# Two-block kernel: the context's norm spread over the second feed-forward layer, its root taken with Ln and Exp

## Chip, cores and metric

One Trainium2 chip, one core of it. The metric is the device time of one execution in microseconds (us), the median over several runs.

## What is computed

One launch computes two model blocks behind each other: a first block of two layers (a retention mixer and a feed-forward layer, then a recurrent mixer and a feed-forward layer) and a second block (state-space mixer with a Fourier branch, then a mixture of experts). The feed-forward layers and the context's norm, which the change touches, are these:

```python
def swiglu_ffn(x, w_in, w_out):
    gate, up = jnp.split(x @ w_in, 2, axis=-1)
    return (jax.nn.silu(gate) * up) @ w_out
...
def rmsnorm(u, w):
    uf = u.astype(jnp.float32)
    uf = uf * lax.rsqrt(jnp.mean(uf * uf, axis=-1, keepdims=True) + EPS)
    return uf.astype(u.dtype) * w

def modulate(u, shift, scale):
    return u * (1 + scale) + shift
...
        prj_c = modulate(rmsnorm(ctx, norm1[layer]), sh1c, sc1c) @ w_in[layer]
```

The sequence and the context have 256 tokens each, the model width is 1024, the feed-forward width 2816 (22 tiles of 128 rows each for gate and for up).

## The kernel before, in words

Each engine has its program written out by hand, and the engines meet at semaphores. Activations lie transposed: the width on the 128 partitions in eight tiles, the 256 tokens as columns. SyncE streams the weights through a ring of 2 MB slots.

**Split products.** An fp32 product is made of three passes. For each chunk of weights (128x1024, eight 128x128 blocks) ScalarE rounds it to `w_hi` (`weights_hi`, line 1545), VectorE forms the remainder `w_lo` (`weights_lo`, line 2038), and TensorE multiplies hi by hi, hi by lo and lo by hi. There are three sets of `w_hi` and `w_lo`: the rounding of chunk n waits until TensorE is done with chunk n-3. In the feed-forward layers one chunk is one 128-row tile of the output.

**The feed-forward layer** (`ffn` in each engine's program: lines 913, 1628 and 2220). The products of `w_in` go to PSUM in 22 out tiles of 128x512, `TILE["ffn_in1", 0]` to `21`, two chunks each, over six banks: the even ones are gates, the odd ones ups. For each pair j, VectorE reads the gate tile 2j out of PSUM, makes two remainders, reads the up tile 2j+1, multiplies it by the gate's Silu (`act<-act,work`), copies the product to `hid_hi` (`CAST`), forms `hid_lo`, and goes on with two more remainders. ScalarE does the Silu of pair j and then the roundings of the next four chunks. Each read of a tile raises `bank_read` of its bank. The first eight chunks' worth of tiles (0 to 3) come out together at the start, the products looping over the input there (`outer_gemm`).

**The context.** GpSimd squares the context `cx` (128x2048) and adds the eight tiles of squares up (lines 641 to 646), in four instructions that start when the sums of squares of the layer's input are done. In the second layer TensorE sums over the partitions with a product by ones in front of chunk 14, ScalarE takes a `Sqrt` ahead of the Silu of pair 4 (line 1633), VectorE a reciprocal ahead of the gate of pair 5 (line 2229), and GpSimd multiplies `cx` by it, four instructions in a row (line 650). ScalarE applies scale and shift and rounds (`context_hi`, line 1618) at pairs 6 to 9, and GpSimd forms the remainders `ctx_lo` behind it (line 653). The context's products come after the feed-forward layer.

The lines of the instructions in the trace are those of helpers: 690 for every product, 1455 for ScalarE, 2001 for VectorE's tensor_tensor.

Of the kernel before, what the change touches and what calls it, by code (L numbers as in the profile page):

```python
# [35 lines left out]
ALU = mybir.AluOpType  # L36
# [3 lines left out]
P = 128  # L40
T = 256
# [197 lines left out]
def two_blocks(nc, a, out):  # L239

    ctx = ExitStack()
    with ctx:
# [54 lines left out]
        def col(name, i=0, n=1, rows=P):  # L297
            return vec[0:rows, VOFF[name][0] + i:VOFF[name][0] + i + n]
# [57 lines left out]
        def xs_both(m):  # L356
# [60 lines left out]
            "ones_set", "csil_zero", "csil_ready", "w_hi_ready", "w_lo_ready", "chunk_used", "in_hi_ready", "in_lo_ready",  # L417
            "sq_ready", "osq_ready", "osum_ready", "sum_ready", "silu_ready", "hid_ready", "gy_ready", "pool_ready", "pool_step", "stats_full", "rstd_ready", "scaled_ready", "h_ready", "x_ready", "rope_done",
            "omv_ready", "osd_ready", "pads_zero", "uc_ready", "tap_ready", "lsp_dve", "lsp_act", "a_ready",
            "th_ready", "lsq_arg", "lsq_ready", "g_done", "go_hi_ready", "go_ready", "mod_full", "wt_ready", "ctx_sum", "ctx_full", "ctx_dev", "ctx_rstd", "ctx_v", "ctx_w", "ctx_hi_ready", "ctx_lo_ready", "coef_ready", "wdt_hi_ready", "wdt_lo_ready", "center_ready", "x_mod",  # L420
            "dt_dve", "dt_act", "dt_ready", "xw_ready", "xd_ready", "rl_ready", "cl_ready", "ce_ready", "dec_ready",
            "m_ready", "y_ready", "exp_arg", "exp_ready", "msk_ready", "count_full", "route_ready", "moe_init",
            "eq_ready", "sgb_ready", "gath_full", "xg_ready", "sg_full", "sgt_ready", "sc_full", "sc_free", "gu_full", "gs_ready",
# [183 lines left out]
        def _(pool):  # L607
            steps = [0]

            def settle(x):  # L610

                x.then_inc(s["pool_step"], 1)
                steps[0] += 1
                pool.wait_ge(s["pool_step"], steps[0])

            def sum_squares(i):

                for j in range(1, 4):
                    pool.wait_ge(s["sq_ready"], 4 * i + j + 1)
                    settle(pool.tensor_tensor(out=sq2[:, 0:2, :], in0=sq2[:, 0:2, :], in1=sq2[:, 2 * j:2 * j + 2, :],  # L620
                                              op=ALU.add))
                pool.tensor_tensor(out=sq2[:, 0, :], in0=sq2[:, 0, :], in1=sq2[:, 1, :], op=ALU.add).then_inc(
                    s["sum_ready"], 1)
# [13 lines left out]
            for j in range(KL):  # L637
                await_read(pool, TILE["lru_u", j] if j < KL // 2 else TILE["lru_y", j - KL // 2])
                v = upad[:, 2 * j:2 * j + 2, LPAD:] if j < KL // 2 else gy[:, 2 * j - KL:2 * j - KL + 2, :]
                pool.tensor_tensor(out=v, in0=v, in1=rstd2, op=ALU.mult).then_inc(s["pool_ready"], 1)  # L640
            pool.wait_ge(s["sum_ready"], 4)
            pool.wait_ge(s["ld_ctx"], 16)
            settle(pool.tensor_tensor(out=sqc, in0=cx, in1=cx, op=ALU.mult))
            settle(pool.tensor_tensor(out=sqc[:, 0:4, :], in0=sqc[:, 0:4, :], in1=sqc[:, 4:8, :], op=ALU.add))
            settle(pool.tensor_tensor(out=sqc[:, 0:2, :], in0=sqc[:, 0:2, :], in1=sqc[:, 2:4, :], op=ALU.add))
            pool.tensor_tensor(out=sqc[:, 0, :], in0=sqc[:, 0, :], in1=sqc[:, 1, :], op=ALU.add).then_inc(s["ctx_sum"], 1)
            pool.wait_ge(s["ctx_rstd"], 1)
            for j in range(4):
                c2 = cx[:, 2 * j:2 * j + 2, :]
                pool.tensor_tensor(out=c2, in0=c2, in1=lnb.unsqueeze(1).to_broadcast([P, 2, T]), op=ALU.mult).then_inc(s["ctx_v"], 1)  # L650
            for j in range(4):
                pool.wait_ge(s["ctx_hi_ready"], 2 * j + 2)
                pool.tensor_tensor(out=ctx_lo[:, 2 * j:2 * j + 2, :], in0=cx[:, 2 * j:2 * j + 2, :],
                                   in1=ctx_hi[:, 2 * j:2 * j + 2, :].bitcast(F32), op=ALU.subtract).then_inc(s["ctx_lo_ready"], 1)
            sum_squares(4)
            pool.wait_ge(s["mod_full"], len(MOD_GROUPS))
            pool.dma_start(wr[0], a["wroute"][:, 0:4, :]).then_inc(s["ld_route"], 16)
# [19 lines left out]
        def _(pe):  # L677
# [233 lines left out]
            next_input(1, "ffn_in0", (1,))  # L911

            def ffn(layer):
                split_gemm(f"ffn_in{layer}", 14, KD, in_hi, in_lo, first_m=BPC)
                if layer:
                    pe.wait_ge(s["ctx_sum"], 1)
                    mm(ps[:, STAT, T:2 * T], ones[:, :], sqc[:, 0, :], True, True, s["ctx_full"])
                split_gemm(f"ffn_in{layer}", 2 * KF, KD, in_hi, in_lo, first_m=14)
                split_gemm(f"ffn_out{layer}", KD, KF, hid_hi, hid_lo,
                           lambda c: pe.wait_ge(s["hid_ready"], KF // 2 * layer + c // 2 + 1))  # L920

# [529 lines left out]
        def _(act):  # L1451
            steps = [0]

            def fn(o, i, f, inc=None, **kw):
                x = act.activation(o, i, f, **kw)  # L1455
                if inc is not None:
                    x.then_inc(inc, 1)
                return x
# [169 lines left out]
            def ffn(layer):  # L1628
                for j in range(KF // 2):
                    weights_hi(chunks_by(f"ffn_in{layer}", 2 * j))  # L1630
                    if layer and j == 4:
                        act.wait_ge(s["ctx_full"], 1)
                        fn(lnb, ps[:, STAT, T:2 * T], ACT.Sqrt, s["ctx_dev"], scale=1.0 / D, bias=col("eps"))
                    if layer and 6 <= j < 10:
                        context_hi(j - 6)
                    await_read(act, TILE[f"ffn_in{layer}", 2 * j])
                    fn(act2[:, j % 2, :], act2[:, j % 2, :], ACT.Silu, s["silu_ready"])
                mixer_out(f"ffn_out{layer}", lambda j: weights_hi(chunks_by(f"ffn_out{layer}", j)))
# [352 lines left out]
        def _(dve):  # L1991
# [228 lines left out]
            def ffn(layer):  # L2220
                for j in range(KF // 2):
                    tg, tu = TILE[f"ffn_in{layer}", 2 * j], TILE[f"ffn_in{layer}", 2 * j + 1]
                    hid, hi = cut(act2[:, j % 2, :], 2, T), hid_hi[:, 2 * j:2 * j + 2, :]
                    weights_lo(chunks_by(f"ffn_in{layer}", 2 * j))
                    if layer and j == 2:
                        modulation()
                    if layer and j == 5:
                        dve.wait_ge(s["ctx_dev"], 1)
                        dve.reciprocal(lnb, lnb).then_inc(s["ctx_rstd"], 1)
                    if j == 0:  # L2230
                        dve.wait_ge(s["mod_full"], 2 if layer == 0 else 5)
                        dve.wait_ge(s["rstd_ready"], 4 * layer + 3)
                    await_full(dve, tg)
                    tt(hid, cut(bank(tg), 2, T), rstd2, MUL, bank_read[tg % ROT])
                    weights_lo(chunks_by(f"ffn_in{layer}", 2 * j + 1))
                    await_full(dve, tu)
                    tt(scaled_up, cut(bank(tu), 2, T), rstd2, MUL, bank_read[tu % ROT])
                    await_read(dve, tu)
                    dve.wait_ge(s["silu_ready"], KF // 2 * layer + j + 1)
                    settle(tt(hid, hid, scaled_up, MUL))  # L2240
                    settle(dve.tensor_copy(hi, hid))
                    tt(hid_lo[:, 2 * j:2 * j + 2, :], hid, hi.bitcast(F32), SUB, s["hid_ready"])
                output_squares(1 + 2 * layer, lambda j: weights_lo(chunks_by(f"ffn_out{layer}", j)))
                weights_lo(chunks_by(f"ffn_out{layer}", 3))
# [615 lines left out]
```

## Time and profile before

| | |
|---|---|
| median of 3 runs | 1442.24 us |
| lowest, highest | 1440.04, 1442.87 us |
| the profiled execution's own time | 1440.12 us |
| its span | 1438.3 us |
| mean granted TensorE clock | 0.975 of full |
| TensorE matmul busy | 1308.0 us (91%) |
| VectorE, ScalarE busy | 800.7 us (56%), 609.3 us (42%) |
| GpSimd busy | 86.4 us (6%), 65 instructions |

Busy time is the time in which an engine had an instruction under way. The timelines used below give an instruction's start and length; an instruction that had to wait for something inside the engine shows that wait as length. A number in brackets behind an instruction is the idle time before it and what ended it.

### The profile page before, as it was taken

The numbers are of one execution on the slowest core, as the hardware profiler recorded it, in microseconds if no ns is written. First come the engines' busy times: TensorE is split into PE (matmuls) and PEld (weight loads), VectorE is DVE, ScalarE is ACT, GpSimd is POOL, SyncE is SP. The second block draws the span as 40 slices with busy tenths as digits, with TensorE's granted clock in tenths as the row PEclk, the third lists the DMA queues.
The fourth block names the chain that finished last, engine by engine and source line by source line (L and its number), as shares of the span: only waits on it lengthen the run. The fifth ranks groups of instructions, "written<-read, shape, count | busy, mean of one in ns | idle before, by whom it ended". The sixth has DMA issues, their size and how long they took to land.

```text
span 1438.3 us, 26289 instructions
## 1 busy us (share of the span) xinstructions
PE 1308.0 (91%) x11170; PEld 1108.8 (77%) x11170; DVE 800.7 (56%) x1221; ACT 609.3 (42%) x946; POOL 86.4 (6%) x65
## 2 busy tenths in 40 slices
PE   7999999999999989899999999899977767777867
PEld 7989698999989978899989999688544334444535
DVE  5558847776468577877559796884221111221314
ACT  6553345444456666455446654764211111111112
POOL 2000000000003100221001000410000000000000
PEclk9999999999999999999999999999999999998999
DMA  9654357544574557355453050458999999999996
GB/s 375 244 208 188 157 196 307 190 177 176 199 318 173 190 234 283 135 193 208 178 198 164 27 240 1 162 217 349 421 428 427 427 428 430 430 425 428 427 428 273
DMA packets 30358, 383.31 MB, mean 266 GB/s; under 512 B 3552, under 2 KB 3728, under 8 KB 7216
## 3 DMA queue, kind: packets, MB, share of 16 engines
q1 hardware_dynamic: 29504, 377.72, 64.6%
q0 software_dynamic: 752, 4.11, 0.7%
q8 instruction: 79, 1.29, 0.4%
q14 instruction: 23, 0.19, 0.0%
HBM read 380.77 MB, written 1.05 MB: 265 GB/s over the span
## 4 chain that ended last, share of the span: by engine, by line
PE 55%; DMA 26%; DVE 10%; ACT 5%; issue 2%; SPq 0%; POOL 0%; DVEq 0%; ACTq 0%; POOLq 0%
PE ps L690 55%; DMA ring<-in_experts 25%; DVE w_lo L2001 3%; DVE work L2013 2%; ACT w_hi L1455 2%; ACT work L1455 1%; DVE work L2001 1%; DVE HM L2001 1%; ACT HM L1455 1%; DVE act L2001 1%; ACT L1455 1%; DMA ring<-in_dense 1%; DVE SQ L2007 0%; DVE X L2013 0%; DVE sg_lo L2001 0%
## 5 line engine op out<-in xcount | busy, mean ns | idle before, releaser
L2001 DVE TENSOR_TENSOR w_lo<-ring,w_hi 128x1024 fp32r<-128x1024 f32 (+1 forms) x273 | 341.9, 1262 | 201.8 <-ACT w_hi L1455 201.5
L690 PE MATMUL ps<-in_hi,w_hi 128*128 128x256 f32 x1376 | 389.1, 283 | 16.1 <-DVE w_lo L2001 15.1
L690 PE MATMUL ps<-in_lo,w_hi 128*128 128x256 f32 x1376 | 385.0, 280 | 0.0
L690 PE MATMUL ps<-in_hi,w_lo 128*128 128x256 f32 x1376 | 385.0, 280 | 0.0
L1455 ACT ACTIVATE w_hi<-ring 128x1024 fp32r<-128x1024 f32 (+1 forms) x273 | 286.1, 1053 | 225.8 <-PE ps L690 221.9
L690 PE MATMUL ps<-ring,work 128*32 128x256 f32 (+3 forms) x2520 | 205.6, 461 | 81.9 <-DMA ring<-in_experts 74.4
L690 PEld LDWEIGHTS ps<-in_hi,w_hi 128*128 128x128 f32 x1376 | 261.0, 190 | 22.1 <-issue 17.0
L690 PEld LDWEIGHTS ps<-in_lo,w_hi 128*128 128x128 f32 x1376 | 261.0, 190 | 0.3
L690 PEld LDWEIGHTS ps<-in_hi,w_lo 128*128 128x128 f32 x1376 | 261.1, 190 | 0.0
L690 PEld LDWEIGHTS ps<-ring,work 128*32 128x32 f32 (+1 forms) x2520 | 84.5, 119 | 185.1 <-issue 108.8
L2013 DVE SCALAR_TENSOR_TENSOR X<-ps,mod,X 128x256 f32<-128x256 f32 x136 | 59.0, 479 | 250.2 <-PE ps L690 250.2
L1455 ACT ACTIVATE work<-ps,mod,coef 128x64 f32<-128x64 f32 x136 | 42.1, 413 | 143.2 <-PE ps L690 143.2
L690 PE MATMUL ps<-hid_hi,w_lo 128*128 128x256 f32 x352 | 98.0, 279 | 0.0
L690 PE MATMUL ps<-hid_lo,w_hi 128*128 128x256 f32 x352 | 98.0, 278 | 0.0
L690 PE MATMUL ps<-hid_hi,w_hi 128*128 128x256 f32 x352 | 98.0, 278 | 0.0
L1455 ACT ACTIVATE work<-ps 128x256 f32<-128x256 f32 (+1 forms) x65 | 31.2, 486 | 139.4 <-PE ps L690 122.6
L690 PE MATMUL ps<-work,HM 128*128 128x64 f32 (+1 forms) x568 | 76.8, 293 | 0.8 <-DVE work L2001 0.3
L690 PEld LDWEIGHTS ps<-work,HM 128*128 128x128 f32 x568 | 67.6, 195 | 12.4 <-DVE work L2001 6.7
L690 PEld LDWEIGHTS ps<-hid_hi,w_hi 128*128 128x128 f32 x352 | 66.6, 189 | 0.0
L690 PEld LDWEIGHTS ps<-hid_hi,w_lo 128*128 128x128 f32 x352 | 66.6, 189 | 0.0
L690 PEld LDWEIGHTS ps<-hid_lo,w_hi 128*128 128x128 f32 x352 | 66.5, 189 | 0.0
L1455 ACT ACTIVATE work<-ps,small 128x512 f32<-128x512 f32 (+1 forms) x39 | 21.9, 596 | 100.1 <-PE ps L690 100.0
(291 smaller groups left out, 1884.3 us busy)
## 6 DMA issues: line engine op xcount, KB each, us to landing
ring<-in_experts SPq DMA_DIRECT2D x89, 2048.0 KB, 23.1
ring<-in_dense SPq DMA_DIRECT2D x82, 2048.0 KB, 7.6
ring<-in_experts SPq DMA_DIRECT2D x5, 512.0 KB, 20.8
work<-in_experts SPq DMA_DIRECT2D x1, 2048.0 KB, 13.7
ring<-in_dense SPq DMA_DIRECT2D x3, 512.0 KB, 7.2
spare<-in_experts SPq DMA_DIRECT2D x1, 1536.0 KB, 10.7
cst<-in_ret_cst POOLq DMA_DIRECT2D x1, 1280.0 KB, 12.8
cst<-in_experts SPq DMA_DIRECT2D x1, 1280.0 KB, 6.0
```

What stands on the lines that cost most here:

```text
L690: i = pe.matmul(o, l, r, start=start, stop=stop)
L1455: x = act.activation(o, i, f, **kw)
L2001: i = dve.tensor_tensor(out=o, in0=x, in1=y, op=op)
L2013: i = dve.scalar_tensor_tensor(out=o, in0=x, scalar=sc, in1=y, op0=op0, op1=op1)
```

## The change

GpSimd's squares are made of two tiles of the context at a time, each pair behind VectorE's read of one out tile of the second feed-forward layer (tiles 3, 5, 7 and 8), and added up as they come. The product by ones moves from chunk 14 to chunk 22. ScalarE takes the root as Exp(-0.5 Ln(x)) at pair 7, so that VectorE's reciprocal goes. GpSimd's four scalings stand behind tiles 13, 15, 17 and 19, with a remainder behind each from the second on. ScalarE's `context_hi` steps move from pairs 6 to 9 to pairs 7 to 10.

```diff
-            pool.wait_ge(s["sum_ready"], 4)
             pool.wait_ge(s["ld_ctx"], 16)
-            settle(pool.tensor_tensor(out=sqc, in0=cx, in1=cx, op=ALU.mult))
-            settle(pool.tensor_tensor(out=sqc[:, 0:4, :], in0=sqc[:, 0:4, :], in1=sqc[:, 4:8, :], op=ALU.add))
-            settle(pool.tensor_tensor(out=sqc[:, 0:2, :], in0=sqc[:, 0:2, :], in1=sqc[:, 2:4, :], op=ALU.add))
+            for j in range(4):
+                await_read(pool, TILE["ffn_in1", (3, 5, 7, 8)[j]])
+                c2, q2 = cx[:, 2 * j:2 * j + 2, :], sqc[:, 2 * j:2 * j + 2, :]
+                settle(pool.tensor_tensor(out=q2, in0=c2, in1=c2, op=ALU.mult))
+                if j:
+                    settle(pool.tensor_tensor(out=sqc[:, 0:2, :], in0=sqc[:, 0:2, :], in1=q2, op=ALU.add))
             pool.tensor_tensor(out=sqc[:, 0, :], in0=sqc[:, 0, :], in1=sqc[:, 1, :], op=ALU.add).then_inc(s["ctx_sum"], 1)
...
+            pool.wait_ge(s["ctx_rstd"], 1)
+            for j in range(4):
+                await_read(pool, TILE["ffn_in1", 13 + 2 * j])
+                c2 = cx[:, 2 * j:2 * j + 2, :]
+                pool.tensor_tensor(out=c2, in0=c2, in1=lnb.unsqueeze(1).to_broadcast([P, 2, T]), op=ALU.mult).then_inc(s["ctx_v"], 1)
+                if j:
+                    context_lo(j - 1)
+            context_lo(3)
...
-                split_gemm(f"ffn_in{layer}", 14, KD, in_hi, in_lo, first_m=BPC)
+                split_gemm(f"ffn_in{layer}", 22, KD, in_hi, in_lo, first_m=BPC)
...
-                    if layer and j == 4:
+                    if layer and j == 7:
+                        load_norm_tables()
                         act.wait_ge(s["ctx_full"], 1)
-                        fn(lnb, ps[:, STAT, T:2 * T], ACT.Sqrt, s["ctx_dev"], scale=1.0 / D, bias=col("eps"))
-                    if layer and 6 <= j < 10:
-                        context_hi(j - 6)
+                        settle(fn(lnb, ps[:, STAT, T:2 * T], ACT.Ln, scale=1.0 / D, bias=col("eps")))
+                        fn(lnb, lnb, ACT.Exp, s["ctx_rstd"], scale=-0.5)
+                    if layer and j >= 7:
+                        context_hi(j - 7)
...
-                    if layer and j == 5:
-                        dve.wait_ge(s["ctx_dev"], 1)
-                        dve.reciprocal(lnb, lnb).then_inc(s["ctx_rstd"], 1)
```

`context_lo(j)` is the former remainder: it waits for both roundings of its pair of tiles and subtracts.

GpSimd's instructions for the context, in the program before (`sum_ready` is raised by the sums of squares of the layer's input):

```order
L643 TENSOR_TENSOR work<-cst 128x2048 [waits ld_ctx,sum_ready]
L644 TENSOR_TENSOR work<-work 128x1024 [waits pool_step]
L645 TENSOR_TENSOR work<-work 128x512 [waits pool_step]
L646 TENSOR_TENSOR work<-work 128x256 [waits pool_step]
L650 TENSOR_TENSOR cst<-cst,lr 128x512 [waits ctx_rstd]
L650 TENSOR_TENSOR cst<-cst,lr 128x512 x3
L653 TENSOR_TENSOR ctx_lo<-cst,ctx_hi 128x512 [waits ctx_hi_ready] x4
```

and in the changed one (each `bank_read` is VectorE's read of an out tile):

```order
L645 TENSOR_TENSOR work<-cst 128x512 [waits bank_read2,ld_ctx]
L645 TENSOR_TENSOR work<-cst 128x512 [waits bank_read4,pool_step]
L647 TENSOR_TENSOR work<-work 128x512 [waits pool_step]
L645 TENSOR_TENSOR work<-cst 128x512 [waits bank_read0,pool_step]
L647 TENSOR_TENSOR work<-work 128x512 [waits pool_step]
L645 TENSOR_TENSOR work<-cst 128x512 [waits bank_read1,pool_step]
L647 TENSOR_TENSOR work<-work 128x512 [waits pool_step]
L648 TENSOR_TENSOR work<-work 128x256 [waits pool_step]
L659 TENSOR_TENSOR cst<-cst,lr 128x512 [waits bank_read0,ctx_rstd]
L659 TENSOR_TENSOR cst<-cst,lr 128x512 [waits bank_read2]
L652 TENSOR_TENSOR ctx_lo<-cst,ctx_hi 128x512 [waits ctx_hi_ready]
L659 TENSOR_TENSOR cst<-cst,lr 128x512 [waits bank_read4]
```

The one long product and its folding became seven instructions of 512 columns and one of 256, in four places, and the scalings, which stood behind each other, each have a wait of their own.

ScalarE's instructions around the Silu of pair 7 in the changed program (`act<-act` is the Silu, `lr` holds the root, `cst` the context):

```order
L1463 ACTIVATE w_hi_54<-ring 128x1024 [waits chunk_used,slot_full1]
L1488 ACT_TABLE_LOAD
L1463 ACTIVATE lr<-ps,vec 128x256 [waits ctx_full]
L1463 ACTIVATE lr<-lr 128x256 [waits act_step]
L1463 ACTIVATE cst<-cst,mod,coef 128x256 [waits coef_ready,ctx_v]
L1463 ACTIVATE cst<-cst,mod,coef 128x256
L1463 ACTIVATE ctx_hi<-cst 128x256 [waits ctx_w]
L1463 ACTIVATE ctx_hi<-cst 128x256
L1463 ACT_TABLE_LOAD
L1463 ACTIVATE act<-act 128x512 [waits bank_read1]
L1463 ACTIVATE w_hi_55<-ring 128x1024 [waits chunk_used,slot_full2]
```

Before, the place of pair 7 had only the four `cst` and `ctx_hi` instructions between the rounding and the Silu; both table loads and the root stood alone in front of the Silu of pair 4.

## Rows read from the trace of the kernel before

**Rows 1.** The page's part 1, busy time of each engine

```profile
PE 1308.0 (91%) x11170; PEld 1108.8 (77%) x11170; DVE 800.7 (56%) x1221; ACT 609.3 (42%) x946; POOL 86.4 (6%) x65
```

**Rows 2.** Windows over both feed-forward layers: us, busy of PE, PEld, DVE, ACT, POOL; clock; DMA

```profile
240.00:408.50 168.50, 167.85 (x1447) 167.46 (x1446) 108.67 (x119) 75.63 (x82) 0.00 (x0) 1.00 0.51 194
575.00:748.90 173.90, 169.45 (x1452) 168.42 (x1451) 118.80 (x124) 85.51 (x100) 23.05 (x12) 1.00 0.48 182
```

**Rows 3.** Timeline of POOL in layer 1: start, length, engine, line, operation

```profile
573.26 4.52 POOL L643 TENSOR_TENSOR work<-cst 128x2048 f32<-128x2048 f32 x1 [87.12 <-DVE work L2001]
...
627.56 7.03 POOL L650 TENSOR_TENSOR cst<-cst,lr 128x512 f32<-128x512 f32 x4 [42.55 <-DVE lr L2229]
...
649.25 1.30 POOL L653 TENSOR_TENSOR ctx_lo<-cst,ctx_hi 128x512 fp32r<-128x512 f32 x1 [9.49 <-ACT ctx_hi L1455]
```

**Rows 4.** Timeline of DVE, start of layer 1

```profile
570.59 2.59 DVE L2001 TENSOR_TENSOR work<-work 128x512 f32<-128x512 f32 x4
573.10 11.32 DVE L2001 TENSOR_TENSOR w_lo<-ring,w_hi 128x1024 fp32r<-128x1024 f32 x4
584.34 0.68 DVE L2001 TENSOR_TENSOR act<-ps,lr 128x512 f32<-128x512 f32 x1
```

**Rows 5.** Timeline of DVE, start of layer 0

```profile
235.18 2.60 DVE L2001 TENSOR_TENSOR work<-work 128x512 f32<-128x512 f32 x4
...
245.89 0.68 DVE L2001 TENSOR_TENSOR act<-ps,lr 128x512 f32<-128x512 f32 x1
...
250.87 0.68 DVE L2001 TENSOR_TENSOR work<-ps,lr 128x512 f32<-128x512 f32 x1
251.73 0.69 DVE L2001 TENSOR_TENSOR act<-act,work 128x512 f32<-128x512 f32 x1 [0.17 <-ACT act L1455]
...
261.78 2.35 DVE L2001 TENSOR_TENSOR w_lo<-ring,w_hi 128x1024 fp32r<-128x1024 f32 x2
```

**Rows 6.** The chain of waits: start, length, what; both layers

```profile
258.37 150.11 PE ps L690 x1296
408.47 0.02 issue
...
597.67 25.75 PE ps L690 x219
...
748.91 0.61 ACT SQ L1455
```

**Rows 7.** Timeline of DVE, layer 0 in its steady part

```profile
275.38 0.69 DVE L2001 TENSOR_TENSOR act<-ps,lr 128x512 f32<-128x512 f32 x1 [0.23 <-PE ps L690]
277.71 1.23 DVE L2001 TENSOR_TENSOR w_lo<-ring,w_hi 128x1024 fp32r<-128x1024 f32 x1 [1.65 <-ACT w_hi L1455]
...
280.98 0.69 DVE L2001 TENSOR_TENSOR work<-ps,lr 128x512 f32<-128x512 f32 x1 [0.38 <-PE ps L690]
...
282.43 0.43 DVE L2241 CAST hid_hi<-act 128x512 fp32r<-128x512 f32 x1
...
283.50 1.22 DVE L2001 TENSOR_TENSOR w_lo<-ring,w_hi 128x1024 fp32r<-128x1024 f32 x1
...
286.42 0.69 DVE L2001 TENSOR_TENSOR act<-ps,lr 128x512 f32<-128x512 f32 x1 [0.23 <-PE ps L690]
```

**Rows 8.** Timeline of DVE beside GpSimd's four scalings

```profile
633.36 0.68 DVE L2001 TENSOR_TENSOR work<-ps,lr 128x512 f32<-128x512 f32 x1
```

**Rows 9.** Timeline of ACT in layer 1, pair 4 and then pair 7

```profile
613.39 1.28 ACT L1455 ACT_TABLE_LOAD   x1
614.68 0.47 ACT L1455 ACTIVATE lr<-ps,vec 128x256 f32<-128x256 f32 x1
...
646.37 1.06 ACT L1455 ACTIVATE w_hi<-ring 128x1024 fp32r<-128x1024 f32 x1 [1.67 <-PE ps L690]
647.34 1.08 ACT L1455 ACTIVATE cst<-cst,mod,coef 128x256 f32<-128x256 f32 x2
648.45 0.73 ACT L1455 ACTIVATE ctx_hi<-cst 128x256 fp32r<-128x256 f32 x2
649.80 0.63 ACT L1455 ACTIVATE act<-act 128x512 f32<-128x512 f32 x1 [0.62 <-DVE act L2001]
```

More of the change, by code:

```diff
@@ L419, in two_blocks @@
             "omv_ready", "osd_ready", "pads_zero", "uc_ready", "tap_ready", "lsp_dve", "lsp_act", "a_ready",
-            "th_ready", "lsq_arg", "lsq_ready", "g_done", "go_hi_ready", "go_ready", "mod_full", "wt_ready", "ctx_sum", "ctx_full", "ctx_dev", "ctx_rstd", "ctx_v", "ctx_w", "ctx_hi_ready", "ctx_lo_ready", "coef_ready", "wdt_hi_ready", "wdt_lo_ready", "center_ready", "x_mod",
+            "th_ready", "lsq_arg", "lsq_ready", "g_done", "go_hi_ready", "go_ready", "mod_full", "wt_ready", "ctx_sum", "ctx_full", "ctx_rstd", "ctx_v", "ctx_w", "ctx_hi_ready", "ctx_lo_ready", "coef_ready", "wdt_hi_ready", "wdt_lo_ready", "center_ready", "x_mod",
             "dt_dve", "dt_act", "dt_ready", "xw_ready", "xd_ready", "rl_ready", "cl_ready", "ce_ready", "dec_ready",
@@ L640, in _, with context_lo @@
                 pool.tensor_tensor(out=v, in0=v, in1=rstd2, op=ALU.mult).then_inc(s["pool_ready"], 1)
-            pool.wait_ge(s["sum_ready"], 4)
             pool.wait_ge(s["ld_ctx"], 16)
-            settle(pool.tensor_tensor(out=sqc, in0=cx, in1=cx, op=ALU.mult))
-            settle(pool.tensor_tensor(out=sqc[:, 0:4, :], in0=sqc[:, 0:4, :], in1=sqc[:, 4:8, :], op=ALU.add))
-            settle(pool.tensor_tensor(out=sqc[:, 0:2, :], in0=sqc[:, 0:2, :], in1=sqc[:, 2:4, :], op=ALU.add))
-            pool.tensor_tensor(out=sqc[:, 0, :], in0=sqc[:, 0, :], in1=sqc[:, 1, :], op=ALU.add).then_inc(s["ctx_sum"], 1)
[L647 to L651, printed above, removed]
+            for j in range(4):
[4 more added lines that the diff above has]
+                    settle(pool.tensor_tensor(out=sqc[:, 0:2, :], in0=sqc[:, 0:2, :], in1=q2, op=ALU.add))
+            pool.tensor_tensor(out=sqc[:, 0, :], in0=sqc[:, 0, :], in1=sqc[:, 1, :], op=ALU.add).then_inc(s["ctx_sum"], 1)
+            def context_lo(j):
                 pool.wait_ge(s["ctx_hi_ready"], 2 * j + 2)
@@ L917, in ffn @@
                     mm(ps[:, STAT, T:2 * T], ones[:, :], sqc[:, 0, :], True, True, s["ctx_full"])
-                split_gemm(f"ffn_in{layer}", 2 * KF, KD, in_hi, in_lo, first_m=14)
+                split_gemm(f"ffn_in{layer}", 2 * KF, KD, in_hi, in_lo, first_m=22)
                 split_gemm(f"ffn_out{layer}", KD, KF, hid_hi, hid_lo,
```

## The prediction

> **What bounds the kernel now.** I read the page first, for the engine that is nearest to full: TensorE's matmuls fill 91% of the span, VectorE 56%, GpSimd 6% [rows 1]. So a change to GpSimd's work is worth only what it makes TensorE wait. Then I looked for a control. The first feed-forward layer (layer 0) has the same products as the second (layer 1) and no context work, and the windows over the two differ: 0.65 us without a matmul in layer 0 (168.50 less 167.85), 4.45 us in layer 1 (173.90 less 169.45), both at a granted clock of 1.00 [rows 2]. The 3.8 us between them are about all that can be won, and a change in the steady part, where layer 0 is full, can only lose.
>
> Where layer 1 loses them is read by laying the timelines over each other. Both layers begin with the same four sums on VectorE, at 235.18 and 570.59, so 335.41 apart. The first gate tile is read at 245.89 and at 584.34, now 338.45 apart: **3.04 us** lost [rows 4, 5]. The reason is above the second of these rows: four remainders took 11.32 us where one takes 1.22 [rows 4, 7], beside GpSimd's squares, which begin at 573.26 with one instruction of 4.52 us [rows 3]. The two engines did not slow each other in part; each VectorE instruction stood still until a GpSimd one was over. TensorE takes the chain over at 258.37 and at 597.67, 339.30 apart [rows 6]; the further 0.85 us come with `modulation()`, which VectorE does at pair 2 in layer 1 alone and which stays. From there to the layers' ends, 408.48 (258.37 plus 150.11) and 748.91, the distance grows to 340.43, by 1.13 us more [rows 6]. In this stretch layer 1 has the product by ones, one in 1300, and the reciprocal with the four scalings in 7.03 us [rows 3]; I put **0.8 us** down to the latter (0 to 1.1).
>
> **What the change takes away.** The burst at the start, 3.04, and what comes of the reciprocal and of the second burst, 0.80, together 3.8 us. The order of the layer's products is as before, and the product by ones costs the same at chunk 22 as at 14: its sum is ready a tile and more ahead.
>
> **What it adds, step by step.** The unit is one GpSimd instruction of 128x512, 1.30 us when nothing holds it up [rows 3]; a step of two is 2.6. What a delay of VectorE costs depends on how far its remainder is ahead of TensorE. A gate tile comes every 11.04 us (275.38 to 286.42) for four chunks, so a chunk is 2.76.
>
> Tile 3, one instruction. In layer 0 VectorE reads this tile at 250.87, then waits 0.17 us for the Silu and multiplies at 251.73 [rows 5]. GpSimd is released by the same read, starts in that gap and holds the multiply for 1.3 less 0.17. Up to 258.37 the chain is made of VectorE and ScalarE work, without slack: **1.1 us**.
>
> Tile 5, two. The remainder behind it starts at 261.78 [rows 5] and is over at 263.0; TensorE wants it two chunks after 258.37, at 263.9. Slack 0.9, cost **1.7**.
>
> Tile 7, two, in the steady part. From 283.50 plus 1.22 to TensorE's next tile at 286.40 [rows 7] the slack is 1.7: cost **0.9**.
>
> Tile 8, three, behind a gate. Here VectorE idles 1.65 us before its next remainder [rows 7], which starts 2.33 after the read. GpSimd's first two end 2.0 after it, and with the lateness left from tile 7 a little is lost: **0.2** (0 to 0.5).
>
> Pair 7 on ScalarE. Count from the rounding that starts at 646.37, when TensorE has just finished the chunk three before [rows 9]. TensorE wants the next pair's first remainder three chunks later, at 8.3. Now stand behind each other: this rounding 1.06, table 1.28, Ln 0.47, Exp taken alike 0.47, GpSimd's first scaling 1.30 (ScalarE waits for it in `context_hi`), scale and shift 1.11, roundings of the context 0.73, table 1.28, Silu 0.63, rounding 1.06, remainder 1.23 [rows 7, 9]. That is 10.6; records of instructions that follow each other overlap by a tenth. TensorE waits **2.3 us**. Before, pair 4 had two tables and the root there, 3.0 us, within the wait for the gate, and pairs 6 to 9 the context's 1.8 (1.11 and 0.73) alone; together, and with GpSimd's 1.3 in the middle, they no longer fit.
>
> Tile 15, two (a scaling and a remainder). After that stall VectorE makes its second remainder until 11.7 and needs 3.7 from the up tile's read to the next remainder's end (280.98 to 283.50 plus 1.22 [rows 7]), so 15.4 against TensorE's 10.6 plus two chunks, 16.1: slack 0.7, cost **1.9**. Tiles 17 and 19, two each, as tile 7: **1.8**. The last remainder falls alone behind pair 10's roundings: nothing, up to 0.3.
>
> Two costs the trace does not show. First, whether GpSimd holds the `CAST` in VectorE's chain, 0.43 us [rows 7]. A read of PSUM beside a scaling kept its 0.68 [rows 8], so some are free; every one that works between SBUF tiles was held [rows 4]. The cast is of that kind, so I take it as held. If free, the five steps of two behind up tiles cost 0.4 less each. The Trainium skill (SBUF — State Buffer, Who interferes with whom) names copies and casts among the operations that can take the port pair shared with GpSimd, and a VectorE operation with two SBUF inputs too; no row here shows it for a cast. By the page the sum stands at the first value, against it at 2.1 us less. Second, which engine wins where both ask at once: either order ends with both GpSimd instructions in front of the same remainder, so I give it nothing.
>
> Sum: 1.1 + 1.7 + 0.9 + 0.2 + 2.3 + 1.9 + 1.8 = 9.9, less 3.8, is **6.1 us slower**. What follows the layer is released by it and starts that much later, the experts' loads too, so nothing absorbs it. The profiled execution took 1440.12 (span 1438.3), near the lowest of the runs and 2.1 under their median of 1442.24; the four times have a mean of 1441.3, and I add to that: **1447.4 us**. 0.2%, 2.9 us, is about what a measurement of this kernel can tell from no change.
>
> **The rivals.**
> *The cast runs free.* 6.1 less 2.1, so 4.0 slower, 1445.3. For it: some VectorE reads were not held. Against: those read PSUM.
> *Only the serial places cost.* The steps behind up tiles find cover (TensorE has more in hand than my 1.7), and tile 3 and pair 7 are what is left: 1.1 + 2.3 - 3.8, 0.4 faster, 1440.9. For it: four scalings in a row and a reciprocal, some 8.8 us, cost just 0.8 before. Against: that burst fell largely on a wait of VectorE, not into the multiply, cast, subtract, remainder chain.
> *Faster: ScalarE's sequence at pair 7 is covered as well.* The place is the remainder of chunk 32, the price 2.3, and the point is whether the slack there exceeds 4.2 us (the 2.0 in the rows and the 2.3). Then 1.1 - 3.8, 2.7 faster, 1438.6; with tile 3 hidden too, 1437.5. For it: pair 4's two tables and root cost no visible stall. Against: three sets of remainders let VectorE be three chunks ahead, 8.3 us, and no more.
> *Lateness adds up* from tile 15 to 19 because VectorE does not catch up between: 3 us more, 1450.4.
>
> **How the numbers follow.** Forecast 0.45, free cast 0.18, only the serial places 0.16, faster 0.16, adding up 0.05. Slower by over 0.2%: 0.45 + 0.05 and most of the free cast, 0.14, is 0.64. Within: the rest of it and nearly all of the serial case, 0.04 + 0.15, 0.19. Faster: 0.16 + 0.01, 0.17. The range leaves out the fastest case and the slowest: 1439.0 to 1450.0.
>
> **What would show it.** In the changed profile: the first gate tile 335.4 after layer 0's; the multiply behind tiles 3, 5, 7, 15, 17 and 19 at 1.0 us or longer, or the cast at 1 and more, and waits of TensorE for `w_lo` behind each; a wait of over 2 us for the remainder after pair 7's Silu, with GpSimd's first scaling in the middle of ScalarE's sequence. I am wrong if layer 1 shows less than 4 us of TensorE idle, or if the context's instructions keep their 1.30 us while the chain beside them keeps its lengths.

## The result, and the profile after

| | before | changed |
|---|---|---|
| median of 11 runs | 1440.44 us | 1444.27 us |
| lowest, highest | 1440.04, 1442.87 | 1442.78, 1446.22 |
| span of the profiled execution | 1438.3 | 1442.7 |
| mean granted clock | 0.975 | 0.973 |

The ratio is 1.0024, with a 95% interval of 1.0016 to 1.0031: the change makes the kernel **3.8 us slower**. The kernel before, run again beside the changed one, has a median 1.8 us under that of its first three runs.

The page's part 1 of the changed kernel, against [rows 1]: every busy time is within 3 us of the one before, so the page says nothing of where the time went.

```profile
PE 1310.9 (91%) x11170; PEld 1110.1 (77%) x11170; DVE 801.6 (56%) x1220; ACT 610.1 (42%) x947; POOL 85.6 (6%) x69
```

One ruler serves for the whole study: the distance from VectorE's four sums, with which a feed-forward layer begins, to ScalarE's last square behind it (`ACT SQ`). In layer 1 that was 178.32 us before (748.91 less 570.59 [rows 4, 6]), and is now 753.22 less 571.08, **182.14**, 3.8 more. In layer 0 it is 173.31 before (408.49 less 235.18) and 173.20 now (408.81 less 235.61). All of the loss lies in layer 1.

The window over layer 1 says the same. Columns: us, busy of PE, PEld, DVE, ACT, POOL; clock; DMA share; GB/s. TensorE is without a matmul for 6.8 us (178.20 less 171.38), 4.45 before [rows 2], at a granted clock of 1.00. So 2.4 of the 3.8 us show as idle time. Part of the rest is pace: behind a stop, the next 48 matmuls take 5.95 or 5.83 us in the chain below, where the steady pace (96 matmuls in 11.04 us [rows 7]) gives 5.52. A stop in this layer costs some 0.3 to 0.4 us beyond its idle time; no run here tells why. The distance above, from start to start, has both in it and is the safer reading.

```profile
575.00:753.20 178.20, 171.38 (x1454) 169.87 (x1453) 119.53 (x123) 86.15 (x101) 23.88 (x16) 1.00 0.47 179
```

**What was won.** VectorE at the start of the layer, against [rows 4]: start, length, operation. The remainders are free of the burst, and the first gate is read 10.62 us behind the sums (581.70 less 571.08), 13.75 before: 3.13 won. At 587.89 the step behind tile 3 holds the multiply for 0.52 (1.21 less 0.69; the 0.52 in its brackets is another thing, the idle time before it, in which it waited for the Silu). Behind tile 5 the cast takes 1.15 and `hid_lo` 1.67, where they take 0.43 and 0.69 alone (583.88, 584.34). The last line is the same multiply in the kernel before: there, too, it waited 0.52 for the Silu, and not the 0.17 of layer 0 that the prediction went by.

```profile
571.08 2.60 DVE L2011 TENSOR_TENSOR work<-work 128x512 f32<-128x512 f32 x4
...
581.70 0.68 DVE L2011 TENSOR_TENSOR act<-ps,lr 128x512 f32<-128x512 f32 x1
...
583.88 0.43 DVE L2248 CAST hid_hi<-act 128x512 fp32r<-128x512 f32 x1
584.34 0.69 DVE L2011 TENSOR_TENSOR hid_lo<-act,hid_hi 128x512 fp32r<-128x512 f32 x1
...
587.89 1.21 DVE L2011 TENSOR_TENSOR act<-act,work 128x512 f32<-128x512 f32 x1 [0.52 <-ACT act L1463]
...
597.90 1.15 DVE L2248 CAST hid_hi<-act 128x512 fp32r<-128x512 f32 x1
599.08 1.67 DVE L2011 TENSOR_TENSOR hid_lo<-act,hid_hi 128x512 fp32r<-128x512 f32 x1
```

```profile
590.52 0.69 DVE L2001 TENSOR_TENSOR act<-act,work 128x512 f32<-128x512 f32 x1 [0.52 <-ACT act L1455]
```

**What was given back.** GpSimd in the changed kernel, against [rows 3]. A squaring alone lasts 1.04 us, an addition or a scaling alone 1.29 or 1.30. Released by an up tile's read, a squaring lasts 1.48 and a scaling 1.80. The scaling of 657.59 ends at 659.39, 1.16 behind the end of VectorE's multiply (657.54 plus 0.69), which began just ahead of it: GpSimd, too, stands still while VectorE works.

```profile
587.51 1.04 POOL L645 TENSOR_TENSOR work<-cst 128x512 f32<-128x512 f32 x1 [100.95 <-DVE work L2011]
597.28 1.48 POOL L645 TENSOR_TENSOR work<-cst 128x512 f32<-128x512 f32 x1 [8.73 <-DVE work L2011]
...
648.44 1.30 POOL L659 TENSOR_TENSOR cst<-cst,lr 128x512 f32<-128x512 f32 x1 [29.15 <-ACT lr L1463]
657.59 1.80 POOL L659 TENSOR_TENSOR cst<-cst,lr 128x512 f32<-128x512 f32 x1 [7.85 <-DVE work L2011]
659.35 1.48 POOL L652 TENSOR_TENSOR ctx_lo<-cst,ctx_hi 128x512 fp32r<-128x512 f32 x1
```

ScalarE at pair 7, against [rows 9]. The sequence is the predicted one, each duration within 0.1: rounding, table, Ln, Exp, a wait of 1.41 for GpSimd's scaling, scale and shift, context roundings, table, Silu, rounding.

```profile
645.06 1.06 ACT L1463 ACTIVATE w_hi<-ring 128x1024 fp32r<-128x1024 f32 x1 [1.66 <-PE ps L698]
646.14 1.28 ACT L1488 ACT_TABLE_LOAD   x1
647.44 0.47 ACT L1463 ACTIVATE lr<-ps,vec 128x256 f32<-128x256 f32 x1
647.94 0.42 ACT L1463 ACTIVATE lr<-lr 128x256 f32<-128x256 f32 x1
649.77 1.10 ACT L1463 ACTIVATE cst<-cst,mod,coef 128x256 f32<-128x256 f32 x2 [1.41 <-POOL cst L659]
650.90 0.72 ACT L1463 ACTIVATE ctx_hi<-cst 128x256 fp32r<-128x256 f32 x2
651.64 1.28 ACT L1463 ACT_TABLE_LOAD   x1
652.94 0.63 ACT L1463 ACTIVATE act<-act 128x512 f32<-128x512 f32 x1
653.47 1.99 ACT L1463 ACTIVATE w_hi<-ring 128x1024 fp32r<-128x1024 f32 x2
```

TensorE has its longest wait there, 2.75 us idle and 3.03 from one matmul's start to the next, where the pace in front of it is 0.12:

```profile
652.89 0.28 PE L698 MATMUL ps<-in_hi,w_lo 128*128 128x256 f32 x1
655.92 0.36 PE L698 MATMUL ps<-in_hi,w_hi 128*128 128x256 f32 x1 [2.75 <-DVE w_lo L2011]
```

The chain of waits (start, length, what), against [rows 6]: before, it left TensorE once in the steady part, from 623.42 (597.67 plus 25.75) until `637.61 111.28 PE ps L690 x960`. Now it leaves it four times, at pair 7 and at tiles 15, 17 and 19.

```profile
602.03 11.42 PE ps L698 x96
...
613.47 31.51 PE ps L698 x267
...
648.44 1.31 POOL cst L659
...
658.27 1.42 DVE hid_hi L2248
659.71 1.67 DVE hid_lo L2011
...
662.66 5.95 PE ps L698 x48
...
674.48 5.83 PE ps L698 x48
...
686.18 67.02 PE ps L698 x576
753.22 0.61 ACT SQ L1463
```

VectorE reads the gate of pair 7 at 647.76, and at 649.08 in the kernel before. Up to there the changed kernel is ahead by 1.8 us, counted from the sums; from there to the layer's end it takes 105.46 us where the kernel before took 99.83, 5.6 more.

### The profile page after: what moved, and what is told of

The parts are those of the page before. It is cut to its first block, busy times and chain, and to the rows that moved or that the text cites. A ratio compares the mean times of both kernels' runs of the same rounds, so it can differ in the third digit from the quotient of the medians.

```text
span 1442.7 us, 26297 instructions
## 1 busy us (share of the span) xinstructions
PE 1310.9 (91%) x11170; PEld 1110.1 (77%) x11170; DVE 801.6 (56%) x1220; ACT 610.1 (42%) x947; POOL 85.6 (6%) x69
## 3 DMA queue, kind: packets, MB, share of 16 engines
q8 instruction: 79, 1.29, 0.4%
## 4 chain that ended last, share of the span: by engine, by line
PE 56%; DMA 26%; DVE 10%; ACT 5%; issue 2%; POOL 0%; SPq 0%; DVEq 0%; ACTq 0%; POOLq 0%
PE ps L698 56%; DMA ring<-in_experts 25%; DVE w_lo L2011 3%; DVE work L2023 2%; ACT w_hi L1463 1%; ACT work L1463 1%; DVE work L2011 1%; DVE act L2011 1%; ACT HM L1463 1%; DVE hid_lo L2011 1%; ACT L1463 1%; DVE HM L2011 1%; DVE hid_hi L2248 0%; DVE SQ L2017 0%; DVE sg_lo L2011 0%
## 5 line engine op out<-in xcount | busy, mean ns | idle before, releaser
L2011 DVE TENSOR_TENSOR w_lo<-ring,w_hi 128x1024 fp32r<-128x1024 f32 (+1 forms) x273 | 334.8, 1237 | 205.7 <-ACT w_hi L1463 205.4
L698 PE MATMUL ps<-in_hi,w_hi 128*128 128x256 f32 x1376 | 389.4, 283 | 19.0 <-DVE w_lo L2011 17.8
L698 PE MATMUL ps<-in_lo,w_hi 128*128 128x256 f32 x1376 | 385.1, 280 | 0.0
L698 PE MATMUL ps<-in_hi,w_lo 128*128 128x256 f32 x1376 | 385.1, 280 | 0.0
L698 PEld LDWEIGHTS ps<-in_hi,w_hi 128*128 128x128 f32 x1376 | 260.9, 190 | 25.4 <-issue 21.7
L698 PE MATMUL ps<-ring,work 128*32 128x256 f32 (+3 forms) x2520 | 206.5, 462 | 80.5 <-DMA ring<-in_experts 73.4
L698 PEld LDWEIGHTS ps<-in_lo,w_hi 128*128 128x128 f32 x1376 | 260.9, 190 | 0.3
L698 PEld LDWEIGHTS ps<-in_hi,w_lo 128*128 128x128 f32 x1376 | 260.9, 190 | 0.0
L698 PEld LDWEIGHTS ps<-ring,work 128*32 128x32 f32 (+1 forms) x2520 | 84.8, 119 | 184.7 <-issue 110.0
L698 PE MATMUL ps<-hid_hi,w_lo 128*128 128x256 f32 x352 | 98.0, 278 | 0.0
L698 PE MATMUL ps<-hid_lo,w_hi 128*128 128x256 f32 x352 | 98.0, 278 | 0.0
L698 PE MATMUL ps<-hid_hi,w_hi 128*128 128x256 f32 x352 | 98.0, 278 | 0.0
L698 PE MATMUL ps<-work,HM 128*128 128x64 f32 (+1 forms) x568 | 76.7, 293 | 0.8 <-DVE work L2011 0.4
L698 PEld LDWEIGHTS ps<-work,HM 128*128 128x128 f32 x568 | 67.5, 195 | 12.4 <-DVE work L2011 6.7
L698 PEld LDWEIGHTS ps<-hid_hi,w_hi 128*128 128x128 f32 x352 | 66.6, 189 | 0.0
L698 PEld LDWEIGHTS ps<-hid_hi,w_lo 128*128 128x128 f32 x352 | 66.6, 189 | 0.0
L698 PEld LDWEIGHTS ps<-hid_lo,w_hi 128*128 128x128 f32 x352 | 66.5, 189 | 0.0
## 6 DMA issues: line engine op xcount, KB each, us to landing
spare<-in_experts SPq DMA_DIRECT2D x1, 1536.0 KB, 10.6
```

Of the source, the lines that this page charges most:

```text
L698: i = pe.matmul(o, l, r, start=start, stop=stop)
L2011: i = dve.tensor_tensor(out=o, in0=x, in1=y, op=op)
```

## The experiments

The theory before them: two GpSimd instructions behind the read of an up tile stand in front of VectorE's short chain and cost up to 1.3 us a step; pair 7 is overfull on ScalarE. The rival: the loss is pair 7's alone, or the serial start's, and the steps elsewhere are covered. "Layer 1" is the distance on the ruler above in the profiled execution; the times are medians beside the kernel before in the same series, which was 1440.49 for the first four and 1441.58 for the next four.

| | layer 1 | against changed | median | ratio to before |
|---|---|---|---|---|
| before | 178.32 | -3.82 | 1440.44 | 1 |
| changed | 182.14 | 0 | 1444.27 | 1.0024 [1.0016, 1.0031] |
| squares in one burst | 183.72 | +1.58 | 1444.33 | 1.0030 [1.0021, 1.0040] |
| roundings a pair later | 176.32 | -5.82 | 1438.53 | 0.9982 [0.9972, 0.9992] |
| squares behind gates | 180.34 | -1.80 | 1441.48 | 1.0007 [0.9998, 1.0016] |
| all behind gates | 174.50 | -7.64 | 1436.28 | 0.9968 [0.9957, 0.9979] |
| remainders later | 181.00 | -1.14 | 1443.19 | 1.0018 [1.0009, 1.0027] |
| root at pair 6 | 178.54 | -3.60 | 1441.57 | 1.0010 [0.9996, 1.0025] |
| Sqrt and reciprocal | 174.92 | -7.22 | 1435.33 | 0.9968 [0.9955, 0.9982] |
| squares behind later ups | 181.56 | -0.58 | 1443.16 | 1.0012 [1.0000, 1.0025] |

**The squares back in one burst** (`e1_sq_burst`). The rest of the change stays.

```diff
-            for j in range(4):
-                await_read(pool, TILE["ffn_in1", (3, 5, 7, 8)[j]])
...
+            pool.wait_ge(s["sum_ready"], 4)
+            settle(pool.tensor_tensor(out=sqc, in0=cx, in1=cx, op=ALU.mult))
+            settle(pool.tensor_tensor(out=sqc[:, 0:4, :], in0=sqc[:, 0:4, :], in1=sqc[:, 4:8, :], op=ALU.add))
+            settle(pool.tensor_tensor(out=sqc[:, 0:2, :], in0=sqc[:, 0:2, :], in1=sqc[:, 2:4, :], op=ALU.add))
```

> The changed kernel with the squares as before: one burst of four instructions behind the input's sums; root, scalings and everything else as changed. In the changed trace the burst's 3.1 us at the start are gone and the squaring steps cost about 1.8 (tile 3 0.5, tile 5 1.0, tile 7 0.3). Theory of places with these sizes: 1.3 us slower than the changed kernel, about 1445.6. With the sizes of the prediction (3.9 us for the steps behind tiles 3, 5, 7 and 8) it would be 0.8 faster, 1443.5.

Measured: 1.58 us more in the layer. Up to GpSimd's first scaling it is 1.34 (649.82 less 571.12 is 78.70, against 77.36); the rest came in a stretch in which TensorE's clock was low, of which more below. So of the 3.13 us that the steps save at the start, the steps themselves use up about 1.8. The timed runs are too coarse to show it: the two ratios to before, 1.0030 and 1.0024, differ by less than their intervals.

**The context's roundings a pair later** (`e2_hi_later`). GpSimd's first scaling then no longer stands inside ScalarE's sequence of pair 7.

```diff
-                    if layer and j >= 7:
-                        context_hi(j - 7)
+                    if layer and j >= 8:
+                        context_hi(j - 8)
...
+                if layer:
+                    weights_hi(CHUNK_AT["ffn_out1"][0] + 3)
+                    context_hi(3)
```

> The changed kernel with ScalarE's context steps one pair later (pairs 8, 9, 10 and one behind the third rounding of the output product), so that pair 7 holds the tables and the root alone and ScalarE no longer waits for GpSimd's first scaling there. Theory of ScalarE's serial sequence: the wait of TensorE of 2.5 us at pair 7 goes, and 0.6 of what tile 15 costs, since VectorE is not late there: 1441.2. Rival, that the port alone costs time and the sequence only shows where VectorE is late anyway: no change, 1444.3.

Measured: 5.82 us less, nearly twice what was expected. Pair 7's wait is gone, and so are the three at tiles 15, 17 and 19. The chain shows one piece to the layer's end:

```profile
601.33 11.42 PE ps L698 x96
...
612.78 133.90 PE ps L698 x1154
...
746.70 0.60 ACT SQ L1463
```

GpSimd's rows say why. With its rounding a pair later, the remainder is not ready when its scaling is, waits 3 us for ScalarE and falls beside the next gate's read. The steps behind up tiles hold one instruction:

```profile
653.43 1.80 POOL L659 TENSOR_TENSOR cst<-cst,lr 128x512 f32<-128x512 f32 x1 [4.59 <-DVE work L2014]
658.24 1.43 POOL L652 TENSOR_TENSOR ctx_lo<-cst,ctx_hi 128x512 fp32r<-128x512 f32 x1 [3.01 <-ACT ctx_hi L1463]
```

VectorE has the cast held as before, and `hid_lo` free:

```profile
654.11 1.40 DVE L2251 CAST hid_hi<-act 128x512 fp32r<-128x512 f32 x1
655.55 0.69 DVE L2014 TENSOR_TENSOR hid_lo<-act,hid_hi 128x512 fp32r<-128x512 f32 x1
```

So one held instruction in the chain of an up tile costs nothing here, the second does. Which part of the gain is pair 7's and which the steps', this run can't tell; the one with the later remainders does.

**The squares behind gates** (`e3_sq_gates`), three pairs later so that the start of the layer, which is serial, is over; the product by ones moves to chunk 28.

```diff
-                await_read(pool, TILE["ffn_in1", (3, 5, 7, 8)[j]])
+                await_read(pool, TILE["ffn_in1", (6, 8, 10, 12)[j]])
...
-                split_gemm(f"ffn_in{layer}", 22, KD, in_hi, in_lo, first_m=BPC)
+                split_gemm(f"ffn_in{layer}", 28, KD, in_hi, in_lo, first_m=BPC)
```

> The changed kernel with the four squaring steps behind gate tiles 6, 8, 10 and 12 instead of tiles 3, 5, 7 and 8, and the product by ones in front of chunk 28; the root stays at pair 7. Behind a gate VectorE waits 1.65 us for ScalarE and its next remainder has 1.9 us of slack. Theory of places: the steps' 1.8 us go, 1442.5. Rival, that a step holds up VectorE's remainders alike wherever it stands: no change, 1444.3.

Measured: 1.80 less. The chain has TensorE in one piece from the start of the steady part to pair 7, `594.65 48.15 PE ps L698 x411`. This is the whole price of the steps behind tiles 3, 5, 7 and 8, seen from the other side than in the first run.

**Everything behind gates** (`e4_all_gates`): the two edits above, and the scalings behind tiles 14, 16, 18 and 20.

```diff
-                await_read(pool, TILE["ffn_in1", 13 + 2 * j])
+                await_read(pool, TILE["ffn_in1", 14 + 2 * j])
```

> e3 and e2 together, and the scalings behind gate tiles 14, 16, 18 and 20 as well. Theory of places: nothing of the context's work is left on the chain, so 7.4 us less than the changed kernel, 1436.9, which is 3.5 less than before. Rival, that two GpSimd instructions behind a gate still delay the remainder beyond its slack: about 0.5 us for each of the seven steps is left, 1440.4.

Measured: 7.64 less, the sum of the two (5.82 and 1.80), and 4.2 us under the kernel before in the timed runs. The chain is unbroken from the steady part's start:

```profile
594.30 150.54 PE ps L698 x1298
...
744.86 0.60 ACT SQ L1463
```

GpSimd is not held either. A scaling and a remainder behind a gate keep their 1.30 us:

```profile
656.83 1.31 POOL L659 TENSOR_TENSOR cst<-cst,lr 128x512 f32<-128x512 f32 x1 [9.68 <-DVE act L2014]
658.09 1.30 POOL L652 TENSOR_TENSOR ctx_lo<-cst,ctx_hi 128x512 fp32r<-128x512 f32 x1
```

They fall into VectorE's idle time before a remainder (1.65 us [rows 7]); what is left over holds that remainder where TensorE is not waiting for it. Layer 1 is now 1.2 us longer than layer 0, of which 0.85 are `modulation()`'s.

**The remainders behind the layer's last gate** (`e5_lo_later`): steps of one behind tiles 15, 17 and 19, and pair 7 as in the change. This separates the two effects of the second run.

```diff
-                if j:
-                    context_lo(j - 1)
-            context_lo(3)
+            await_full(pool, TILE["ffn_out1", 0])
+            for j in range(4):
+                context_lo(j)
```

> The changed kernel with the four remainders of the context moved behind the input product (they wait for the first out tile of the output product), so that the steps behind tiles 15, 17 and 19 hold one GpSimd instruction each instead of two. Theory of slack: one instruction holds VectorE's chain for 1.0 us, under the 1.65 of slack, two hold it for 2.0. Tile 15 still falls behind the stall at pair 7 and keeps about 0.3 of its 1.3, tiles 17 and 19 lose their 0.8 and 0.7: 2.5 us less than the changed kernel, 1441.8. Rival, that every hold costs its length: half of 2.8 us goes, 1442.9.

Measured: 1.14 less. The order of things is as expected, with one wait of TensorE left, 2.8 us at pair 7, and TensorE in one piece behind it. That piece is too long for its work: 96.34 us for 816 matmuls, where the kernel before needs 111.28 for 960 (0.1159 each), so 94.6 for these.

```profile
655.16 96.34 PE ps L698 x816
```

The windows show where. For 8 us behind the wait the granted clock is 0.79, and in the middle of it 0.50, the 1.2 GHz level. Ahead of it TensorE had stood still for 2.75 us, in the first of the three windows:

```profile
648.00:656.00 8.00, 5.25 (x46) 5.08 (x46) 2.21 (x2) 6.01 (x9) 0.98 (x1) 1.00 0.02 6
656.00:664.00 8.00, 8.00 (x57) 8.00 (x57) 6.57 (x8) 4.10 (x8) 1.78 (x1) 0.79 0.70 264
657.00:659.00 2.00, 2.00 (x11) 2.00 (x11) 1.93 (x3) 0.00 (x0) 1.62 (x1) 0.50 0.66 262
```

The 1.7 us that are too many (96.34 less 94.6) and the 1.14 won make 2.9. Of these, 0.2 lie ahead of GpSimd's first scaling (77.15 behind the sums, 77.36 in the changed kernel), where the two programs are the same. That leaves some 2.7 us for the second instruction in the three steps, expected 2.5.

**The same again** (`e10_lo_later_again`), one execution, to see whether the low clock was chance.

> The kernel of the run with the four remainders behind the layer's last gate, once more, for its clock. Theory A: the stretch of 8 us with a granted clock of 0.79 right behind the 2.9 us wait of TensorE was chance of that one execution; the same stretch then shows about 1.00 here, and the layer from VectorE's sums to ScalarE's last square takes about 1.6 us less than its 181.0 us, some 179.4. Theory B: the clock falls there each time with this order of the work; 0.79 again, and 181.0 us.

Measured: 180.79 us, and 1442.26 us in all beside 1442.02. The fall came again, at 0.86 in the same window and 0.93 in the one before; the piece of 816 took 95.94. So theory A did not come out here; two executions alone do not separate it from theory B.

**The changed kernel again** (`e11_change_again`), one execution.

> The changed kernel once more, for its clock behind the long wait of pair 7. Theory A (the fall of the clock belongs to the execution, not to the order of the work): one look in several shows a granted clock under 0.9 in the first 8 us after that wait, here too at times. Theory B (it belongs to the kernel): 1.00 there, as in the first profile, and 182.1 us from VectorE's sums to ScalarE's last square.

Measured: the layer took 182.38 us (752.99 less 570.61), and the clock fell here too, where it had been 1.00 in the first profile:

```profile
656.00:664.00 8.00, 8.00 (x59) 8.00 (x58) 7.65 (x8) 3.94 (x7) 3.22 (x2) 0.80 0.70 264
```

So theory B fails: the same program shows both, and the fall belongs to the execution. The fall cost this execution only 0.2 us: TensorE, at the lower clock, had not yet run out of remainders when tile 15's step was over, and the chain goes straight through (`655.44 12.94 PE ps L698 x96`).

**The burst again** (`e12_burst_again`), one execution.

> The kernel with the squares in one burst, once more. Theory A: the clock of 0.79 in its 8 us after the wait of pair 7 was this one execution's; now 1.00. Theory B: 0.8 again, as the kernel with the later remainders showed twice. Either way the layer up to GpSimd's first scaling takes 78.7 us from VectorE's sums.

Measured: 183.47 us, with 1.00 in the window where the first execution had 0.79, and 78.68 up to GpSimd's first scaling. Without the fall the burst costs 1.33 more than the steps, as expected (1.3). Its time in all was 1446.87, beside 1441.49: from the layer's last square to the end it took 691.4 (1445.1 less 753.72), 687.5 in the first execution (1442.3 less 754.84), so that difference lies behind the layer.

**The root at pair 6** (`e6_root_pair6`): both tables, Ln and Exp a pair ahead of the first `context_hi`.

```diff
-                    if layer and j == 7:
+                    if layer and j == 6:
                         load_norm_tables()
```

> The changed kernel with the tables, Ln and Exp one pair earlier (pair 6) and the context's steps as changed, pairs 7 to 10: the two halves of ScalarE's sequence no longer stand behind each other, and GpSimd's first scaling is over when pair 7 asks for it. The steps behind tiles 15, 17 and 19 keep two instructions. Theory of the serial sequence: the 2.5 us at pair 7 go and 0.8 of the 1.3 at tile 15, 3.3 less than the changed kernel, 1441.0. Rival, that the later place of the remainders was what the kernel with ScalarE's steps a pair later gained by: under 1 us, 1443.5.

Measured: 3.60 less. ScalarE has both tables and the root at 634.22 to 637.75, and TensorE does not wait there. The second piece of the chain reaches the step of tile 15, and the steps of two are left, 5.95 and 5.83 apart as in the change:

```profile
612.60 39.71 PE ps L698 x338
...
658.18 5.95 PE ps L698 x48
...
670.01 5.83 PE ps L698 x48
...
681.71 67.02 PE ps L698 x576
```

**Sqrt and reciprocal** (`e8_sqrt_recip`): "all behind gates" with the former root, Sqrt at pair 7 and the reciprocal behind the read of gate 14.

```diff
-                        load_norm_tables()
                         act.wait_ge(s["ctx_full"], 1)
-                        settle(fn(lnb, ps[:, STAT, T:2 * T], ACT.Ln, scale=1.0 / D, bias=col("eps")))
-                        fn(lnb, lnb, ACT.Exp, s["ctx_rstd"], scale=-0.5)
+                        fn(lnb, ps[:, STAT, T:2 * T], ACT.Sqrt, s["ctx_dev"], scale=1.0 / D, bias=col("eps"))
...
+                    if layer and j == 7:
+                        dve.wait_ge(s["ctx_dev"], 1)
+                        dve.reciprocal(lnb, lnb).then_inc(s["ctx_rstd"], 1)
```

> The kernel with all steps behind gates (e4), but with the root as before: Sqrt on ScalarE at pair 7 and VectorE's reciprocal, 1.75 us, behind its read of gate tile 14, where it waits for ScalarE anyway. Theory of places: the reciprocal fits into that gap, so no difference from e4 beyond 0.5 us, 1436.5. Rival, that the reciprocal was what cost before: 1.7 slower than e4, 1438.0.

Measured: layer 1 0.42 longer than with Ln and Exp, TensorE's waits the same 1.3 us in both, the ratio to before the same 0.9968. The reciprocal takes 1.74 us in VectorE's idle time. How the root is taken makes no difference that these runs can tell.

**The squares behind later up tiles** (`e9_sq_later_ups`), where nothing is serial any more.

```diff
-                await_read(pool, TILE["ffn_in1", (3, 5, 7, 8)[j]])
+                await_read(pool, TILE["ffn_in1", (7, 9, 11, 12)[j]])
```

and the product by ones at chunk 28, as above.

> The changed kernel with the squaring steps behind up tiles 7, 9 and 11 and gate tile 12, in the steady part, instead of 3, 5, 7 and 8; the product by ones in front of chunk 28. Theory: the 0.5 and 1.0 us of tiles 3 and 5 go, since there the chain has little or no slack; each step of two behind an up tile in the steady part holds the chain for 1.7 us against 1.65 and costs 0.1 to 0.3. In all 1.0 less than the changed kernel, 1443.3. Rival, that up tiles are bad wherever they stand: no less, 1444.3 or more.

Measured: 0.58 less in the layer instead of 1.0. The steps of two behind up tiles cost again, and a cost came that was not foreseen: TensorE reached the product by ones before GpSimd's last square, addition and folding were done, and the chain runs through them.

```profile
636.24 1.05 POOL work L645
...
637.36 1.30 POOL work L647
...
638.72 1.62 POOL work L648
...
640.38 3.66 PE ps L698 x27
```

## Why the prediction was right in direction and too large

The sign, the mechanism and the places were right; the size was not: 6.1 us were forecast and 3.8 measured. The step that failed is the **unit**: "one GpSimd instruction of 128x512, 1.30 us when nothing holds it up [rows 3]; a step of two is 2.6". That is how long GpSimd's instruction lasts, not how long it holds VectorE. Read as VectorE's extra length, a squaring held the next instruction for 0.72 us (cast 1.15 for 0.43), an addition, scaling or remainder for 0.98 (cast 1.41 for 0.43, `hid_lo` 1.67 for 0.69). A step of two cost VectorE 1.70 or 1.96 us, where 2.6 was taken. In order:

| term | predicted | measured | from |
|---|---|---|---|
| burst at the start, removed | 3.04 | 3.13 | first gate behind the sums |
| reciprocal and four scalings, removed | 0.80 | about 0.5 | rest of the 1.8 up to pair 7 |
| tile 3 | 1.1 | 0.5 | multiply held 0.52 |
| tile 5 | 1.7 | 1.0 | held 1.70, slack 0.7 |
| tile 7 | 0.9 | 0.3 | chain, 11.42 for 11.04 |
| tile 8 | 0.2 | 0 | no wait |
| pair 7 on ScalarE | 2.3 | 2.9 | 3.03 from matmul to matmul, less 0.12 |
| tile 15 | 1.9 | 1.2 | 655.92 to 662.66, less 5.52 |
| tiles 17 and 19 | 1.8 | 1.5 | chain, 11.82 and 11.70 for 11.04 |
| sum | +6.1 | +3.8 | |

The last three terms make 5.6, as the distance from pair 7's gate to the layer's end does (105.46 less 99.83). The 0.5 of the second row is what the others leave of the 1.8 ahead of that gate, and no run took it alone.

The unit does not explain all, and the sum is nearer than its terms deserve. With the holds as measured and everything else as predicted, tile 3 would cost about 0.6, tile 5 0.8, tile 7 nothing, tile 8 nothing, tile 15 1.3 and tiles 17 and 19 together 0.5; with pair 7's 2.3 and less the 3.8 won, that is 1.7 us slower. Three things put 2.1 back. Pair 7 cost 0.6 more than predicted. Each stop of TensorE costs 0.3 to 0.4 beyond the wait, for which the prediction had no term: at tile 17, 0.45 us show as idle (8.00 less 7.55 in the window 672 to 680), but the stretch is 0.8 too long. And the 3.8 won were 3.6. So tiles 17 and 19 came nearly right, 1.5 for 1.8, by two errors against each other; that is luck. Tile 3's term had an error of its own besides: the multiply's wait for the Silu was read from layer 0, 0.17, where layer 1 had 0.52 before the change too.

The first run bears out the start as a whole (1.3 us net won by the steps), the third the steps behind tiles 3 to 8 (1.80, against 3.9 predicted and 1.8 in the table), the remainders' run the second instruction in three steps (2.7, the clock's part counted in).

- **The cast.** The rival "the cast runs free" falls: 0.43 became 1.15 and 1.41. The Trainium skill (SBUF — State Buffer, Who interferes with whom) says that a cast can take the port pair that VectorE shares with GpSimd, and the trace agrees. The same section has the loser stand still for the whole instruction; taken as GpSimd's length in the trace, that was too much by a third, 1.30 for 0.98. The measurement decides.
- **Pair 7.** The order came out as predicted, with Exp 0.05 shorter, and TensorE started again 10.86 us behind the rounding (655.92 less 645.06), 10.6 predicted. It had run out at 8.0 (652.89 less 645.06, and one matmul more), not at 8.3, so the price was 2.9. The rival "covered as well" falls.
- **Only the serial places cost** falls too: the first gate, tile 3 and pair 7 alone would have given a gain of 0.4, and tiles 15 to 19 alone cost 2.7.
- **Lateness adds up** did not happen: 1.2, then 0.8 and 0.7.
- **The level.** I took 1441.3 for the kernel before, from four times; eleven gave 1440.44. The direction of the timed ratio does not hang on it.
- **What follows the layer** starts later and catches nothing up, as said: the loss in the layer, 3.82, is the loss in the median.
- **The signs.** The first gate tile came 335.40 behind layer 0's (581.70 less 246.30), and the held multiply and casts and the wait at pair 7 were there. But "less than 4 us of TensorE idle" could hardly have spoken against the prediction: the kernel before has 4.45 [rows 2].
- **What was not weighed.** The prediction treats the place behind an up tile as given. That one instruction there is free and the second is not, and that a gate's read has room for two, was in its own rows: 1.65 us of idle time behind the gate [rows 7], and slack 1.7 in the steady part against one hold, whether taken as 1.30 or as 0.98.

## What to carry to other kernels

When a helper engine's instructions hold up an engine that the chain runs through, as GpSimd's held VectorE here, put them behind the read that is followed by idle time, not behind the read that opens a dependent chain: the steps cost 4.5 us placed mostly behind up tiles (the table's steps without pair 7), and next to nothing behind gates. Count how many of them stand in one step, not how many there are; the first used up the slack, the second was paid for. And before a sequence with table loads is put in one place, add up what the next engine has in stock: Ln, Exp and both tables fitted a pair earlier, or without GpSimd's scaling in the middle.

## What was unexpected of the hardware

- **The hold is shorter than the instruction**, and it goes both ways. GpSimd's 1.30 us held VectorE for 0.98, and its own instruction grew to 1.80 where it was issued under VectorE's multiply. With both queues full the two took turns: multiply, scaling, cast, remainder, `hid_lo`.
- **A product of one tile by itself is shorter on GpSimd**: 1.04 us for 128x512, and 1.29 to 1.31 with two different operands.
- **TensorE's clock can fall behind a short wait.** Behind the wait of 2.75 us at pair 7 (2.5 in the run with the squares behind later up tiles) the granted clock went to 0.79, 0.79, 0.86 and 0.80 over 8 us in four profiled executions, down to 0.50 (1.2 GHz) over 2 us; in four others with the same wait it stayed at 1.00. The changed kernel and the burst each showed both. In the five executions without such a wait (before, roundings a pair later, all behind gates, root at pair 6, Sqrt and reciprocal) it never fell in this layer. It cost about 1.35 and 1.75 us where nothing absorbed it, and 0.2 where the wait at tile 15 came right behind (182.38 and 182.14 in the changed kernel, 183.72 and 183.47 in the burst). What decides between the two stays open; no run here tells it.
